# A triangular inverse's cross products on four array tiles, brought back by ScalarE's copies

## What is computed

```python
def step(S, inp):
    r_t, w_t, k_t, v_t, kk_t, a_t = inp
    sa = jnp.einsum('bhvk,bhk->bhv', S, -kk_t)
    S = (S * w_t[:, :, None, :]
         + sa[..., None] * (kk_t * a_t)[:, :, None, :]
         + v_t[..., None] * k_t[:, :, None, :])
    y = jnp.einsum('bhvk,bhk->bhv', S, r_t)
    return S, y
```

## Time and profile before

| | us |
|---|---|
| median of 3 runs | 2953.13 |
| lowest, highest | 2949.37, 2953.44 |
| profiled execution | 2955.44 |
| its span | 2953.6 |
| the rounds with the inverse | some 590 to 1030 |
| TensorE busy | 2894.0 |
| ScalarE busy | 1000.5 |
| VectorE busy | 1590.1 |

### The profile page before, as it was taken

The page is one execution under the profiler, slowest core; times in us unless marked ns, Lnnn a source line. Parts: engine busy times, 40 slices in busy tenths (PEclk is TensorE's granted clock), DMA queues, the critical chain, the costliest instruction groups (busy, mean ns, idle before and its releaser), DMA issues.

```text
span 2953.6 us, 56334 instructions
## 1 busy us (share of the span) xinstructions
PE 2894.0 (98%) x23722; PEld 2461.5 (83%) x23722; DVE 1590.1 (54%) x2062; ACT 1000.5 (34%) x1740; POOL 1484.9 (50%) x1070
## 2 busy tenths in 40 slices
PE   8999999999999999999999999999999999999998
PEld 7888888888888879987888888787998788888887
DVE  7331633377777632339666644544234966674453
ACT  4122312244554522325333322231333433332222
POOL 4554543456666544276544433556426654553344
PEclk9999999999999999999999999999999999999999
DMA  4533356422232231112333356344111223336632
GB/s 159 186 111 97 122 164 191 148 67 53 57 79 68 66 104 37 51 50 84 111 128 142 122 214 236 134 143 157 43 44 43 100 111 125 142 121 228 228 143 86
DMA packets 175572, 346.56 MB, mean 117 GB/s; under 512 B 46816, under 2 KB 104352, under 8 KB 169696
## 3 DMA queue, kind: packets, MB, share of 16 engines
q1 hardware_dynamic: 175328, 343.06, 34.2%
HBM read 240.24 MB, written 102.76 MB: 116 GB/s over the span
## 4 chain that ended last, share of the span: by engine, by line
PE 48%; DVE 3%; issue 1%; DMA 1%; POOL 1%; ACT 0%; DVEq 0%; SPq 0%; ACTq 0%; POOLq 0%
PE ps L2259 29%; PE ps L1697 14%; PE ps L2211 3%; DMA w_raw<-in_weights 1%; DVE normed L3185 0%; DVE t_raw L2879 0%; POOL sumsq L853 0%; PE ps L2417 0%; DVE t_raw L2887 0%; POOL sq L851 0%; DVE rstd L2429 0%; PE ps L2231 0%; DVE t_lo L2893 0%; POOL w_lo L833 0%; DVE normed L3211 0%
## 5 line engine op out<-in xcount | busy, mean ns | idle before, releaser
L833 POOL TENSOR_TENSOR w_lo<-w_raw,w_hi 128x512 fp32r<-128x512 f32 x232 | 334.9, 1467 | 504.3 <-ACT w_hi L1138 500.6
L1697 PE MATMUL ps<-a_hi,w_hi 128*128 128x512 f32 x1140 | 446.0, 391 | 10.5 <-DVE a_lo L2439 10.0
L1697 PE MATMUL ps<-a_lo,w_hi 128*128 128x512 f32 x1140 | 444.7, 390 | 0.0
L1697 PE MATMUL ps<-a_hi,w_lo 128*128 128x512 f32 x1140 | 351.8, 390 | 0.0
L1138 ACT ACTIVATE w_hi<-w_raw 128x512 fp32r<-128x512 f32 x228 | 129.9, 623 | 623.9 <-PE ps L1697 481.4
L2259 PE MATMUL ps<-a_hi,w_hi 128*128 128x512 f32 x800 | 313.8, 392 | 12.5 <-ACT p_t L1524 4.9
L2259 PE MATMUL ps<-a_lo,w_hi 128*128 128x512 f32 x800 | 312.4, 390 | 0.0
L2259 PE MATMUL ps<-a_hi,w_lo 128*128 128x512 f32 x800 | 312.3, 390 | 0.0
L1697 PEld LDWEIGHTS ps<-a_hi,w_hi 128*128 128x128 f32 x1140 | 214.6, 188 | 55.4 <-DVE a_lo L2439 10.0
L1697 PEld LDWEIGHTS ps<-a_hi,w_lo 128*128 128x128 f32 x1140 | 214.6, 188 | 44.8
L1697 PEld LDWEIGHTS ps<-a_lo,w_hi 128*128 128x128 f32 x1140 | 214.7, 188 | 44.1 <-issue 0.2
(11 more groups left out here) (381 smaller groups left out, 6392.0 us busy)
## 6 DMA issues: line engine op xcount, KB each, us to landing
w_raw<-in_weights SPq DMA_DIRECT2D x228, 512.0 KB, 4.1
hidden<-hid SPq DMA_DIRECT2D x44, 1024.0 KB, 3.9
zT<-z_out SPq DMA_DIRECT2D x44, 512.0 KB, 3.4
a_hi<-hidden SPq DMA_DIRECT2D x44, 512.0 KB, 8.4
a_lo<-hidden SPq DMA_DIRECT2D x44, 512.0 KB, 9.6
w_raw<-kvw SPq DMA_DIRECT2D x32, 512.0 KB, 3.3
suv<-zT SPq DMA_DIRECT2D x16, 512.0 KB, 4.5
x<-in_xT SPq DMA_DIRECT2D x16, 512.0 KB, 5.7
```

The lines of the kernel that those rows point to most:

```text
L833: pool.tensor_tensor(low_t[:, part, :], w_raw[:, u, part, :], high[:, part, :].bitcast(F32), ALU.subtract).then_inc(S["w_lo_done"], 1)
L1697: mm = pe.matmul(to[:, nb, 0:w], wt[:, k, :], r[:, k, nb * w:(nb + 1) * w], start=(k == 0 and r is hi_in and wt is high), stop=(k == kn - ...
```

## The change

The halves of each step are now the two values of e in place of the parity of m: `turned`, `take_level`, `evac_x` and `merge` work on e = 0 in bank 0 and on e = 1 in bank 1, and `xm` is laid out by e and m. In `cross` the heads of e = 0 go from lane a to lane a, and those of e = 1 from lane a to the other lane (`a ^ e`), so that four successive products use four tiles. `cross` waits for both transposes first, and its order is m, e, a; the signal for e = 0 comes with the third last product, that for e = 1 with the last. `evac_x` copies e = 0 with one ACTIVATE over 128 partitions and e = 1 with two over 64 partitions each, from one lane to the other (`crossed`): three in place of two. `merge` still uses two tiles. At level 4 `cross` now stands ahead of the `turn` of bt on TensorE; ScalarE's order is as before.

```diff
-        xm = rw("xm", [P, 2, 2, 2, C])
+        xm = rw("xm", [P, 2, HP, C])
...
+        def sides(t, e, part, b):
+
+            return t[part, e].rearrange("p m (n two b) -> p (m n) two b", two=2, b=b)
+
+        def blocks_in(bank, at, part, b):
+
+            return ps[part, bank, at:at + L].rearrange("p (n b) -> p n b", b=b)
+
+        def crossed(e):
+
+            if e == 0:
+                return ((slice(0, P), slice(0, P)),)
+            return ((lane(0), lane(1)), (lane(1), lane(0)))
...
-                for g in range(2):
-                    act.wait_ge(S["x_ps"], 10 * n + 2 * lv + g + 1)
-                    act.activation(xm[:, :, g].rearrange("p e m (n two b) -> p e (m n) two b", two=2, b=b)[:, :, :, 0, :],
-                                   ps[:, g, 2 * L:3 * L].rearrange("p (e n b) -> p e n b", e=2, b=b), ACT.Copy).then_inc(S["x_ev"], 1)
+                for e in range(2):
+                    act.wait_ge(S["x_ps"], 10 * n + 2 * lv + e + 1)
+                    for to, frm in crossed(e):
+                        act.activation(sides(xm, e, to, b)[:, :, 0, :], blocks_in(e, 2 * L, frm, b), ACT.Copy).then_inc(S["x_ev"], 1)
...
-                for g in range(2):
-                    pe.wait_ge(S["inv_tr"], 10 * n + 2 * lv + g + 1)
-                    for mh, e, a in by_tile():
-                        t_u = inv_t[lane(a), g, 2 * e + mh, :].rearrange("p (n two b) -> p n two b", two=2, b=b)[:, :, 0, :]
-                        mm = pe.matmul(unit(a, g, 2 * L + e * C + mh * 32, 32), atrb[par][lane(a), e, 2 * mh + g, 0, :], t_u,
-                                       start=True, stop=True)
-                    mm.then_inc(S["x_ps"], 1)
+                pe.wait_ge(S["inv_tr"], 10 * n + 2 * lv + 2)
+                for m, e, a in by_tile():
+                    t_u = inv_t[lane(a), e, m, :].rearrange("p (n two b) -> p n two b", two=2, b=b)[:, :, 0, :]
+                    mm = pe.matmul(unit(a ^ e, e, 2 * L + m * 32, 32), atrb[par][lane(a), e, m, 0, :], t_u, start=True, stop=True)
+                    if (m, a) == (HP - 1, 1):
+                        mm.then_inc(S["x_ps"], 1)
...
-                for g in range(2):
-                    pe.wait_ge(S["x_ev"], 10 * n + 2 * lv + g + 1)
...
+                for e in range(2):
+                    pe.wait_ge(S["x_ev"], 15 * n + 3 * lv + 1 + 2 * e)
...
                 if behind:
+                    cross(b, q, 4)
                     turn(b, bt, "bt_done", (S["sg_vh"], min(b + 2, GROUPS)), 3, "btr")
-                    cross(b, q, 4)
                     merge(b, q, 4)
...
-                    dve.transpose(inv_t[:, g], units(inv[par], g)).then_inc(S["inv_tr"], 1)
+                    dve.transpose(inv_t[:, e], inv[par][:, e]).then_inc(S["inv_tr"], 1)
...
-                for g in range(2):
-                    dve.wait_ge(S["tu_ps"], 10 * n + 2 * lv + g + 1)
-                    take(rights(inv[par], g, b), low[:, lv + 1, 1].rearrange("p (m n b) -> p m n b", m=HP, b=b),
-                         ps[:, g, 0:2 * C].rearrange("p (m n b) -> p m n b", m=HP, b=b), "tu_ev")
+                for e in range(2):
+                    dve.wait_ge(S["tu_ps"], 10 * n + 2 * lv + e + 1)
+                    take(sides(inv[par], e, slice(0, P), b)[:, :, 1, :], low[:, lv + 1, 1].rearrange("p (n b) -> p n b", b=b),
+                         blocks_in(e, 0, slice(0, P), b), "tu_ev")
```

More of the change, by code:

```diff
@@ L1929, in by_tile @@
             def by_tile():
-                return [(mh, e, a) for mh in range(2) for e in range(2) for a in range(2)]
+                return [(m, e, a) for m in range(HP) for e in range(2) for a in range(2)]
             def cross(n, par, lv):
@@ L1937, in cross @@
                     pe.wait_ge(S["ev_b"], 2 * n + 2)
-                for g in range(2):
-                    pe.wait_ge(S["inv_tr"], 10 * n + 2 * lv + g + 1)
-                    for mh, e, a in by_tile():
-                        t_u = inv_t[lane(a), g, 2 * e + mh, :].rearrange("p (n two b) -> p n two b", two=2, b=b)[:, :, 0, :]
-                        mm = pe.matmul(unit(a, g, 2 * L + e * C + mh * 32, 32), atrb[par][lane(a), e, 2 * mh + g, 0, :], t_u,
-                                       start=True, stop=True)
-                    mm.then_inc(S["x_ps"], 1)
+                pe.wait_ge(S["inv_tr"], 10 * n + 2 * lv + 2)
[4 more added lines that the diff above has]
+                        mm.then_inc(S["x_ps"], 1)
             def merge(n, par, lv):
                 b = LEVELS[lv]
-                for g in range(2):
-                    pe.wait_ge(S["x_ev"], 10 * n + 2 * lv + g + 1)
-                    for mh, e, a in by_tile():
-                        u_u = inv[par][lane(a), e, 2 * mh + g, :].rearrange("p (n two b) -> p n two b", two=2, b=b)[:, :, 1, :]
-                        mm = pe.matmul(unit(a, g, e * C + mh * 32, 32), xm[lane(a), e, g, mh, :], u_u, start=True, stop=True)
+                for e in range(2):
+                    pe.wait_ge(S["x_ev"], 15 * n + 3 * lv + 1 + 2 * e)
+                    for m in range(HP):
+                        for a in range(2):
+                            u_u = inv[par][lane(a), e, m, :].rearrange("p (n two b) -> p n two b", two=2, b=b)[:, :, 1, :]
+                            mm = pe.matmul(unit(a, e, m * 32, 32), xm[lane(a), e, m, :], u_u, start=True, stop=True)
                     mm.then_inc(S["tu_ps"], 1)
@@ L2562, in turned @@
             def turned(n, par, lv):
-                for g in range(2):
-                    dve.wait_ge(S["tu_ev"], 11 * n + (2 * lv + g if lv else 1))
-                    dve.transpose(inv_t[:, g], units(inv[par], g)).then_inc(S["inv_tr"], 1)
+                for e in range(2):
+                    dve.wait_ge(S["tu_ev"], 11 * n + (2 * lv + e if lv else 1))
+                    dve.transpose(inv_t[:, e], inv[par][:, e]).then_inc(S["inv_tr"], 1)
             def take_first(n, par):
```

## The result

The changed kernel takes 2973.74 us, the median of 5 runs (2965.91 to 2975.79), against 2952.43 of the kernel before: a ratio of 1.0064 in the record, interval 1.0044 to 1.0084 (the two medians alone give 1.0072). It is slower by some 20 us, beyond the range that was given, and beyond every rival too: the slowest, A, was at 2968. The profiled execution took 2975.8 us, its span is 2974.0 against 2953.6.

A forecast was written before the change was run, and what follows sets the result against it. TensorE, busy 98% of the span, was taken as the bound. Per round -0.44 - 0.18 + 0.56 = -0.06, 14 rounds -0.8, first and last group -0.6: -1.4 us, from 2953.13 to 2951.7; range 2943 to 2965.

The forecast's parts named there:

- A: In cross, the pace doesn't change on four tiles (bank rule, or tiles not really parallel): 2968 us, chance 0.14.
- Change 1: cross on four array tiles: starts 16.5 ns apart instead of 29, 0.39 us less per level, bounds 0 and 0.43.
- Level 1: From solve 1 to turn_gate on TensorE: 0.32 us less, or 0.44 with level 0's part.
- Level 0: From cross(0) to state_out: 0.12 us less, not 0.39, since state_out also needs VectorE's h_st.
- the one on `merge(4)`: At level 4: the stalled merge(4) holds up all of the next round's start on TensorE.
- Levels 2 and 3: From loras to key_scales, with ScalarE late next: 0.18 us less for the two levels, bounds 0 and 0.29.
- One more costs 0.16: The third ACTIVATE per level in evac_x: 0.16 us of ScalarE, from two copies taking 0.44 against 0.28 for one.
- a bound of 0.1 a copy: Copies reading one half of the partitions and writing the other: taken as free, bounds -0.03 and +0.1 us each.
- Rival B: Copies across halves run end to end, or ScalarE's chain doesn't move up: 2959 to 2963 us, chance 0.16.
- Change 4: cross(4) ahead of the transposes of bt: key_scales to merge(4) 3.27 us instead of 2.71, 0.56 lost, bounds 0.50 and 0.65.
- the second half of `merge` finds its copies done: At level 4: its copies come 0.31 us after the first's, against 0.47 of products, so no further wait.

The follow-up runs named there:

- Experiments 1 and 2: 1: changed kernel with cross(4) back behind the transposes of bt, 2959.55 us; kernel before with it ahead, 2976.17. 2: changed kernel with y_b waiting for h_st, 2971.06.
- the old order: The changed kernel with cross(4) put back behind the transposes of bt on TensorE: 2959.55 us, ratio 1.0018.
- experiment 4: The changed kernel with two copies in place (e = 1 results land with the wrong chunk), cross(4) behind the transposes of bt, y_b after h_st: 2947.21 us, ratio 0.9974.

## Why the prediction was wrong

**Change 1, the pace: right.** `cross` takes 0.67 for 32 records: (0.67 - 0.22) / 31 = 14.5 ns apart against 29, which saves 0.45 a level; 0.39 was forecast. The limit was the tiles'. The rule of the Trainium skill (PSUM — Partial Sum Buffer, section PSUM bank collisions raise a hardware error) that the prediction weighed doesn't show in the time: two row tiles in one bank, on different column halves of the array, ran at full pace. Rival A is out.

**Level 1: right in kind**, 0.45 where 0.32 was forecast; the products next to it overlapped no less than before. **Level 0: wrong, and the mechanism was in no case.** I took `h_st` as 0.50 long, as in the earlier trace rows, and moved it with TensorE. That 0.50 holds only while `h_st` starts ahead of `y_b`, by 0.17 us in that round (and is itself 0.08 longer than `h_st` alone, because of `bonus`). The step that failed is the one on `merge(4)`: I wrote that its stall holds up the next round's start on TensorE, and didn't ask which work of other engines stays where it was. +0.58 in place of -0.12, in 13 rounds. The trace of before held a warning that I hadn't looked for: of its rounds one, at 897.8, has an `h_st` of 1.46 us, and there `y_b` came first. Experiments 1 and 2 show it from both sides.

**Levels 2 and 3: the second step that failed, a price used twice.** "One more costs 0.16" came from two copies of the same form. The change's copies have other starts of partitions, and the group goes from 0.44 to 0.86 with the instruction behind them held too: `th` to the end of `v_tok` grew from 7.56 to 8.25, where I had +0.01. For crossing, which no row showed, I had a bound of 0.1 a copy; it isn't the crossing that costs, but the change of the first partition, 0.12 to 0.14 for each held start, the one of `gate` too, which wasn't counted. The end is +0.46 in place of -0.18. Rival B named this mechanism (copies end to end), but put only +0.16 on it.

**Change 4: right**, +0.49 (0.56 forecast) with the idle time of 0.85 ended by `xm`. But "the second half of `merge` finds its copies done" failed for the same reason as above, +0.13.

**What no step had.** TensorE's clock: 7.6 us of the profiled execution. And part of each gain goes back: in undisturbed rounds of the old order levels 0 and 1 are shorter by 0.11 and 0.45, but from a round's start to the last record of `loras` the means over 14 rounds are equal (15.77 us in both). Much of the difference appears as waits of TensorE that the profile puts down to issue (9.9 us in the old order's rounds, 5.8 in before). What those are (the expectations call them the instruction supply, which no run shows), and why the clock falls in some kernels, no experiment settled. It fell in the rounds of all kernels with the new order and four tiles, and once in those of experiment 4, which have the old order; it didn't in the other kernels of the old order, nor in before with the new one. How long TensorE idles doesn't decide it alone: in the windows of 590 to 1030 us, first of experiment 4, then of the old order in the changed kernel, the one that is busy for longer has the fall (granted clock 0.99 and 1.00):

```profile
590.00:1030.00 440.00, 404.72 (x11658) 350.11 (x11652) 319.53 (x709) 220.25 (x522) 274.98 (x265) 0.99 0.25 65
```
```profile
590.00:1030.00 440.00, 398.90 (x11369) 342.63 (x11363) 318.00 (x698) 244.69 (x584) 275.32 (x262) 1.00 0.25 65
```

## What to carry to other kernels

Before a stall is put on one engine, list what the other engines do beside the work behind it, in both orders of start: a duration read from a row holds only for the neighbours that it had there. Price an added instruction from a row with the same first partitions before and behind it, and count its successor's start too. And where each step saves less than half a microsecond, compare means over all rounds, not one steady round: half or more of such a gain came back as waits elsewhere.

## What the runs showed of the hardware

- ScalarE: ACTIVATEs that copy 128 columns from PSUM (0.26 to 0.28 us each) start 0.15 to 0.18 us apart where the first partitions stay, 0.28 to 0.30 where that read or written changes between 0 and 64, over 64 or 128 partitions alike.
- VectorE and GpSimd, one TENSOR_TENSOR each on SBUF: the later one stands. `h_st` of 0.43 us became 1.15, ending 0.29 after `y_b`, and 0.50, ending 0.29 after `bonus`; the other way round `y_b` took 1.47 in place of 1.27.
- TensorE in 64 x 64 tiles: products of 32 columns start 29 ns apart on two tiles and 14.5 on four, with both row halves of the array in one bank, on different column halves.
- In the changed kernel a stretch of 6.8 us at a granted clock of 0.50 (1.2 GHz in place of 2.4) cost 3.0 us.
